# Expert values in two halves: one half of the columns as a dense product, the other gathered

## The reference, cut to what matters

```python
idx = jnp.take_along_axis(cand_idx, pos, axis=-1)      # i1 * 128 + i2
gate = jax.nn.softmax(top_s.astype(jnp.float32), axis=-1).astype(tb.dtype)
u = expert_u[idx]
v = expert_v[idx]
act = jax.nn.gelu(jnp.einsum('td,thkd->thk', tb, u), approximate=False)
return jnp.einsum('thk,thkd->td', gate * act, v)
```

## Time and profile before

| | |
|---|---|
| median of 3 runs | 1885.55 us (1879.7 to 1885.57) |
| profiled execution | 1886.42 us, span 1884.6 us |
| busy: TensorE, VectorE | 81%, 57% of the span |
| busy: GpSimd, ScalarE | 41%, 18% |
| bytes moved | 713 MB, 378 GB/s over the span |
| granted clock of TensorE, mean | 0.983 |

### The profile page before, as it was taken

How to read it: one execution, slowest core, us unless ns; L and a number is a source line. 1 busy time by engine, 2 the same in 40 slices (tenths; PEclk the granted TensorE clock), 3 DMA queues, 4 the chain that set the end, 5 groups by cost and what they waited for, 6 DMA issues and landing times.

```text
span 1884.6 us, 13048 instructions
## 1 busy us (share of the span) xinstructions
PE 1530.9 (81%) x4481; PEld 704.7 (37%) x4481; DVE 1075.2 (57%) x1518; ACT 331.4 (18%) x860; POOL 780.5 (41%) x666
## 2 busy tenths in 40 slices
PE   5989999999999677777777778777777777777775
PEld 3434564565459323223232323232232323232232
DVE  3127888776138846565564655553865555646445
ACT  3011211120122211211212121121221211111111
POOL 0002243311005585545555555452764545455441
PEclk8999999999999899999999999999999999999998
DMA  9998998885657999999999999999999999999997
GB/s 361 360 351 309 336 355 308 321 316 215 226 195 293 372 423 422 421 422 421 422 421 421 421 422 421 421 422 413 414 421 422 422 421 421 421 421 422 421 421 295
DMA packets 145008, 713.04 MB, mean 378 GB/s; under 512 B 14320, under 2 KB 16944, under 8 KB 77616
## 3 DMA queue, kind: packets, MB, share of 16 engines
q0 software_dynamic: 92160, 604.02, 78.2%
q1 hardware_dynamic: 52784, 108.20, 15.7%
HBM read 709.97 MB, written 2.20 MB: 378 GB/s over the span
## 4 chain that ended last, share of the span: by engine, by line
DMA 54%; PE 31%; DVE 6%; POOL 5%; issue 2%; SPq 1%; ACT 1%; DVEq 0%; POOLq 0%; ACTq 0%
DMA arena<-in_expert_v,arena 48%; PE PS L1558 6%; PE PS L1417 6%; POOL arena L505 5%; PE PS L1637 5%; PE PS L1319 5%; DMA arena<-in_expert_u,arena 5%; PE PS L1300 3%; DVE arena L1174 2%; PE PS L1275 1%; DMA arena<-in_w_in 1%; PE PS L1441 1%; DMA arena<-in_w_mod 1%; PE PS L1352 1%; SPq L340 1%
## 5 line engine op out<-in xcount | busy, mean ns | idle before, releaser
L1637 PE MATMUL PS<-arena 128*128 128x512 f32 x2016 | 942.0, 612 | 309.5 <-DMA arena<-in_expert_v,arena 309.5
L1174 DVE CUSTOM_DVE_ANT_0 arena<-arena 128x2048 f32<-128x2048 f32 x256 | 584.3, 2291 | 496.0 <-DMA arena<-in_expert_u,arena 495.4
L1637 PEld LDWEIGHTS PS<-arena 128*128 128x128 f32 x2016 | 368.5, 192 | 882.5 <-DMA arena<-in_expert_v,arena 505.7
L505 POOL DMA_INDIRECT arena<-in_expert_v,arena x256 | 370.0, 1445 | 446.8 <-PE PS L1637 413.3
L505 POOL DMA_INDIRECT arena<-in_expert_u,arena x256 | 313.3, 1224 | 241.7 <-DVE arena L1155 89.2
L798 ACT ACTIVATE arena<-arena 128x128 f32<-128x128 f32 x252 | 98.0, 402 | 770.3 <-PE PS L1637 769.5
L902 DVE SCALAR_TENSOR_TENSOR arena<-arena 128x1024 f32<-128x1024 f32 x120 | 161.1, 1342 | 26.8 <-DMA arena<-in_w_mod 24.0
L434 POOL DMA_DIRECT2D arena<-in_w_mod x128 | 68.6, 538 | 224.1 <-DVE arena L902 194.1
L1417 PE MATMUL PS<-arena 128*128 128x512 f32 x256 | 111.5, 593 | 0.0
L1558 PE MATMUL PS<-arena 128*128 128x512 f32 x256 | 110.9, 593 | 0.4 <-DVE arena L1076 0.4
L1319 PE MATMUL PS<-arena 128*128 128x512 f32 (+1 forms) x256 | 99.5, 547 | 4.2 <-DMA arena<-in_w_in 4.2
(11 more groups left out here) (207 smaller groups left out, 839.0 us busy)
## 6 DMA issues: line engine op xcount, KB each, us to landing
arena<-in_w_mod POOLq DMA_DIRECT2D x128, 512.0 KB, 6.9
arena<-in_w_mod SPq DMA_DIRECT2D x32, 1024.0 KB, 14.3
arena<-in_w_in SPq DMA_DIRECT2D x28, 1024.0 KB, 15.6
arena<-in_w_out SPq DMA_DIRECT2D x16, 1024.0 KB, 12.5
arena<-in_w_query SPq DMA_DIRECT2D x8, 1024.0 KB, 8.5
arena<-in_x SPq DMA_DIRECT2D x4, 1024.0 KB, 6.3
arena<-cum_rows SPq DMA_DIRECT2D x4, 1024.0 KB, 9.1
arena<-tail_rows SPq DMA_DIRECT2D x4, 1024.0 KB, 6.8
```

The costliest lines, as they stand in the source:

```text
L505: nc.gpsimd.indirect_dma_start(slot, None, table, bass.IndirectOffsetOnAxis(ap=idx[:, u % BUF, j:j + 1], axis=0),).then_inc(arrived, 16)
L1174: V.tensor_tensor_reduce(out=rows, in0=rows, in1=h2row[u // PH], scale=1.0, scalar=0.0, op0=ALU.mult, op1=ALU.add, accum_out=dots[:, u % B ...
L1637: ins = M(PS[:, 4 * blk + b, :], diag_slot[j % 8], vslot[m % NV][:, b * NQ:(b + 1) * NQ], start=first, stop=last)
```

## The change

The columns of expert_v are split into two halves of 1024 (4 KB of a row each).

*Right half, units 0 to 13 (224 slots, `N_DENSE`).* It is not gathered. For each token block a matrix G (128 x 128 x 128: first key index on the partitions, second key index i, token t) is built in SBUF. It holds for each expert and token the sum of the coefficients. Then the right half of the whole table is read once in 128 tiles (128 rows, one for each first index, of 4 KB: `tile_load`, by SyncE, four places), and TensorE multiplies each tile with G of both blocks (`all_experts`, four products of 128x512).

G is built for four tokens at a time, 32 batches for each block. For token t GpSimd makes a 0/1 matrix, slot by first key index (`first_halves`, four compares of 128x128), a second one, slot by second key index, holds the coefficient in place of 1, and TensorE multiplies them (`scatter`, one product of 128x128 for each token); ScalarE copies four results into G (`g_out`). The second matrix is made by ScalarE for block 0 (Abs, Relu and Copy with a scale) and by VectorE for block 1. Block 0's batches stand between dot products 146 and 208, one at every second; block 1's stand in one piece behind dot product 223, with coefficients and indices transposed by TensorE ahead of them.

*Left half, units 0 to 13.* Half rows of 4 KB are gathered. 96 of the slots go over TensorE as before, with two products each (86 of them spread from dot product 28 on, 9 for every 4 half rows, ten between block 1's batches, `V_LATE`). The other 128 are gathered in pairs and added by VectorE (`add_row`).

*Units 14 and 15.* Their rows of expert_u are gathered after G is done, in one ring of four places of 8 KB with the pairs; after them their whole rows of expert_v alternate with the other pairs (`ITEMS`). The ring runs beside the tiles. Unit 15 is routed only after block 1's batches.

*Other.* x after the mixing is stored to HBM and loaded again at tile 64; the last steps are rearranged in `close`; the loop of w_mod loads on GpSimd is written out; some semaphores are merged; one small product makes the numbers 1 to 128.

```diff
+HALF = D // 2
+BLK = PH * TOPK
+DENSE = UNITS - 2
+N_DENSE = DENSE * TOPK
+SLOTS = [BLK, N_DENSE - BLK]
+BATCH = 4
+BATCHES = P // BATCH
+V_SLOTS = 4
+TILES = 4
+LAST_TILES = 3
...
+V_SPREAD, V_PE = 86, 96
+V_AT = {n: [m for m in range(V_SPREAD) if 28 + 9 * m // 4 == n] for n in range(N_DENSE)}
+G_AT = {146 + 2 * b: b for b in range(BATCHES)}
+T_AT, T_MORE = 140, 214
+V_LATE = {1: [86, 87, 88, 89], 5: [90], 9: [91], 13: [92], 17: [93], 21: [94], 25: [95]}
+ITEMS = [x for i in range(2 * TOPK) for x in (("u", N_DENSE + i), ("pair", V_PE + 2 * i))]
+ITEMS += [x for i in range(2 * TOPK) for x in (("pair", V_PE + 4 * TOPK + 2 * i), ("full", N_DENSE + i))]
+N_RING = 4
```

The places in SBUF (offset in KB) and SyncE's list:

```diff
+        vslot = [at(64 + 4 * s, HALF) for s in range(V_SLOTS)]
+        bring = [at(k, D) for k in (152, 64, 72, 199)]
+        tile = [at(k, HALF) for k in (191, 195, 172, 178)]
+        acc = [at(168, HALF), at(160, D)]
+        G = [at(k, P * P).rearrange("p (i t) -> p i t", i=P) for k in (80, 0)]
+        oh1, oh2 = [[at(160 + 4 * a + 2 * b, BATCH * P).rearrange("p (t i) -> p t i", t=BATCH) for b in range(2)] for a in range(2)]
```

```diff
+            def tile_load(i):
+                if i == 0:
+                    sp.wait_ge(u_used, U_EARLY)
+                elif i == 2:
+                    sp.wait_ge(idx_ready, UNITS)
+                elif i == 3:
+                    sp.wait_ge(g_ps, 2 * BATCHES)
+                    sp.wait_ge(v_used, V_PE)
+                elif i >= TILES:
+                    sp.wait_ge(tile_used, i - TILES + 1)
+                src = expert_v.rearrange("(a b) n -> a b n", b=NKEYS)[:, i, HALF:D]
+                sp.dma_start(tile[i % TILES], src).then_inc(tile_in[i % TILES], 16)
+            for i in range(NKEYS):
+                tile_load(i)
+                if i == NKEYS // 2:
+                    grow_load(3)
+                    sp.wait_ge(dram_out, 80)
+                    for t in range(2):
+                        sp.dma_start(x1row[t], x1_dram[t * P:(t + 1) * P, :]).then_inc(grow_in, 16)
```

GpSimd:

```diff
             def gather_v(m):
                 if m == 0:
...
+                    pool.wait_ge(dram_out, 80)
+                if m >= V_SLOTS:
+                    pool.wait_ge(v_used, m - V_SLOTS + 1)
...
+            def item_load(k):
...
+                if kind == "pair":
+                    gather(expert_half, slot[:, 0:HALF], arrived, i, idx_left)
+                    gather(expert_half, slot[:, HALF:D], arrived, i + 1, idx_left)
+                else:
+                    gather(expert_u if kind == "u" else expert_v, slot, arrived, i)
+            def first_halves(b):
...
+                used = slice(0, SLOTS[blk])
+                for i in range(BATCH):
+                    ins = nc.gpsimd.tensor_scalar(oh1[b % 2][used, i, :], iota128[used], eT[used, 0, t + i:t + i + 1], None, ALU.is_equal)
+                ins.then_inc(oh1_ready, 1)
...
-            n = 0
-            for m in range(UNITS * TOPK):
-                while n < u_before(m):
-                    gather_u(n)
-                    n += 1
-                gather_v(m)
+            for n in range(N_DENSE):
+                gather_u(n)
+                for m in V_AT[n]:
+                    gather_v(m)
+                if n in G_AT:
+                    first_halves(G_AT[n])
+            item_load(0)
+            for b in range(BATCHES):
+                first_halves(BATCHES + b)
+                for m in V_LATE.get(b, []):
+                    gather_v(m)
+            for k in range(1, len(ITEMS)):
+                item_load(k)
```

ScalarE, block 0's second matrix and the copy into G:

```diff
+            def second_halves(b):
+                act.wait_ge(slots_evac, 2)
+                if b >= 2:
+                    act.wait_ge(g_ps, b - 1)
+                o = oh2[b % 2]
+                for i in range(BATCH):
+                    ins = A(o[:, i, :], iota128, ACT.Abs, bias=eT[:, 1, b * BATCH + i:b * BATCH + i + 1])
+                step(ins)
+                step(A(o, o, ACT.Relu, scale=-1.0, bias=1.0))
+                for i in range(BATCH):
+                    ins = A(o[:, i, :], o[:, i, :], ACT.Copy, scale=coefT[:, b * BATCH + i:b * BATCH + i + 1])
+                ins.then_inc(oh2_ready, 1)
+            def g_out(b):
+                blk, t = divmod(b * BATCH, P)
+                act.wait_ge(g_ps, b + 1)
+                A(G[blk][:, :, t:t + BATCH], PS[:, 6 + b % 2, :].rearrange("p (t i) -> p i t", t=BATCH), ACT.Copy).then_inc(g_evac, 1)
```

VectorE, block 1's second matrix, the adding of rows and the new order:

```diff
+            def second_halves(b):
...
+                    dve.wait_ge(slots_evac, 4)
+                dve.wait_ge(g_ps, b - 1)
+                for i in range(BATCH):
+                    ins = ts(oh2[b % 2][used, i, :], iota128[used], eT[used, 1, t + i:t + i + 1], coefT[used, t + i:t + i + 1],
+                             ALU.is_equal, ALU.mult)
+                ins.then_inc(oh2_ready, 1)
...
+            def add_row(m, row):
+                a = acc[m // BLK]
+                c = coef[:, m:m + 1]
+                if m == V_PE:
+                    dve.wait_ge(v_used, V_PE)
+                    ins = stt(a, row, c, PS[:, 0:2, :].rearrange("p b n -> p (b n)"), ALU.mult, ALU.add)
...
+                else:
+                    ins = stt(a, row, c, a, ALU.mult, ALU.add)
+                ins.then_inc(row_added, 1)
+                dve.wait_ge(row_added, ROWS.index(m) + 1)
+            def item(k):
...
-                if n == (PH + 1) * TOPK - 1:
-                    after_block(0)
-            after_block(1)
+            for b in range(BATCHES, 2 * BATCHES):
+                second_halves(b)
+            pick_keys(UNITS - 1)
+            pick_pairs(UNITS - 1)
+            for k in range(len(ITEMS)):
+                item(k)
...
+            dve.wait_ge(blk_done, 1)
+            close(0)
+            for h in range(2):
+                part = slice(HALF + h * NQ, HALF + (h + 1) * NQ)
+                dve.wait_ge(blk_done, 2 + h)
+                tt(acc[1][:, part], acc[1][:, part], PS[:, 4 + h, :], ALU.add).then_inc(right_added, 1)
+            dve.wait_ge(right_added, 2)
+            close(1)
```

TensorE:

```diff
             def expert_rows(m):
+                pe.wait_ge(v_in[m % V_SLOTS], 16 * (m // V_SLOTS + 1))
+                pe.wait_ge(coef_ready, m + 1)
+                for b in range(2):
+                    ins = M(PS[:, b, :], diag_slot[m % DIAGS], vslot[m % V_SLOTS][:, b * NQ:(b + 1) * NQ], start=(m == 0), stop=(m == V_PE - 1))
                 ins.then_inc(v_used, 1)
...
+            def scatter(b):
+                pe.wait_ge(oh1_ready, b + 1)
+                pe.wait_ge(oh2_ready, b + 1)
+                pe.wait_ge(g_evac, b - 1) if b >= 2 else pe.wait_ge(sc_evac, UNITS)
+                used = slice(0, SLOTS[b // BATCHES])
+                for i in range(BATCH):
+                    ins = M(PS[:, 6 + b % 2, i * P:(i + 1) * P], oh1[b % 2][used, i, :], oh2[b % 2][used, i, :], start=True, stop=True)
+                ins.then_inc(g_ps, 1)
+            def all_experts(i, blk):
+                for h in range(2):
+                    ins = M(PS[:, 2 + 2 * blk + h, :], G[blk][:, i, :], tile[i % TILES][:, h * NQ:(h + 1) * NQ], start=(i == 0), stop=(i == NKEYS - 1))
...
+                return ins
+            for n in range(N_DENSE):
+                if n == T_AT:
+                    slot_transposes(0)
+                    coef_transpose(0)
+                if n == T_MORE:
+                    slot_transposes(1)
+                for m in V_AT[n]:
                     expert_rows(m)
+                if n in G_AT:
+                    scatter(G_AT[n])
+            coef_transpose(1)
+            for b in range(BATCHES):
+                scatter(BATCHES + b)
+                for m in V_LATE.get(b, []):
+                    expert_rows(m)
+            pe.wait_ge(g_evac, 2 * BATCHES)
+            for i in range(NKEYS - LAST_TILES):
+                pe.wait_ge(tile_in[i % TILES], 16 * (i // TILES + 1))
+                all_experts(i, 0)
+                all_experts(i, 1).then_inc(tile_used, 1)
+            for blk in range(2):
+                for i in range(NKEYS - LAST_TILES, NKEYS):
+                    pe.wait_ge(tile_in[i % TILES], 16 * (i // TILES + 1))
+                    all_experts(i, blk)
```

More of the change, by code:

```diff
@@ L41 @@
 GR = 4
-NU = NV = 8
+NU = 8
 EARLY = 5
@@ L89 @@
 FIRST_KEYS_AFTER, FIRST_PAIRS_AFTER, FIRST_WEIGHTS_AFTER = 4, 9, 3
-LAST_ON_DVE = (8, 10, 12, 14)
-LAST_ON_PE = [j for j in range(TOPK) if j not in LAST_ON_DVE]
+WEIGHTS_AFTER = 15
 STATES = [(2, 0), (3, 0), (3, 1), (2, 1), (0, 0), (1, 1)]
@@ L440, in _ @@
                 tail_load(k % MORE_TAILS, 0, k)
-            with pool.Fori(1, 4) as half:
+            for half in range(1, 4):
                 for k in range(KT):
                     pool.wait_ge(tail_used, half * KT + (k - MORE_TAILS + 1))
-                    pool.sem_inc(pool_go, 1)
                     tail_load(k % MORE_TAILS, half, k)
@@ new lines, in _, with square @@
+            for u in range(DENSE):
+                unit(u)
+            coef_out(1)
+            for m in V_LATE[1]:
```

(31 more changed lines are left out.)

341 lines of the change are left out of this document (205 added, 136 removed).

## The result

The change makes the kernel slower: 2013.9 us (2005.3 to 2016.9, 4 runs) against 1885.6 us, a ratio of 1.068 with a 95% interval of 1.064 to 1.072. The forecast had the sign, the place and the two engines, and not the size: 1911 us, range to 1958. The profiled execution has a span of 2013.3 us.

A forecast was written before the change was run, and what follows sets the result against it. The full software DMA queue was taken to bound the kernel. With 98 us less to move (110 saved, 12 for 4 KB pieces) and 124 more idle, it came 25 us slower: 1911 us, own range 1892 to 1945, joined range 1812 to 1958.

The forecast's parts named there:

- Bytes: Whole kernel: about 46 MB or 110 us less to move; 4 KB pieces at about 410 GB/s cost 12 us.
- Stage A: First gather to dot product 28, before any expert_v: starts at 573.4, done at 666 us.
- B1: Dot products 28 to 145: VectorE sets 2.93 us each, against 3.06 of DMA; 346 us, to 1012.
- I take 3.9: Dot products 146 to 207, compares on GpSimd: 3.9 us each, between 3.06 and 4.3; 236 us, to 1248.
- Block 1's batches: Second token block's 32 batches, nothing streamed: compares 72 us, late half rows 28; 100 us, ends 60 and 115.
- The last stage: Tiles beside the ring: 484 us of transfers, ending at 1895; TensorE 443 us, not the bound by 41.
- Rival 2: Last stage, four-slot ring beside the tiles: queue not kept full, 4.3 us an item, +66, 1975 us; chance 0.10.
- Rival 1: GpSimd's compares find gaps in dot products 146 to 207 and block 1's batches: 1826 us; chance 0.40.
- the forecast's signs of being right: Dot products 146 to 207 at 3.7 us or more; batches near 100 us, share under 0.3; then 405 to 415 GB/s.
- B2: Dot products 146 to 207, with compares on GpSimd: 4.3 us each as upper end, 3.9 taken, 236 us.

The follow-up runs named there:

- e2: The kernel after, with block 0's compares made by VectorE instead of GpSimd: 1914.9 us.
- e1: The kernel after, with VectorE summing the row of expert_u alone (one SBUF input, not two) for dot products 146 to 207: 1958.4 us.
- e7: e2 with two of the four first compares of each block 1 batch moved from GpSimd to VectorE: 1899.9 us.
- e8: The kernel after with the edits of e2, e5, e6 and e7 together: 1871.8 us, ratio 0.995 to the kernel before.
- e5: e2 with all 96 half rows gathered before dot product 224, none between block 1's batches: 1892.1 us.
- e4: The kernel after, with small extra products on TensorE into an unused bank to keep it busy: 2008.9 us.
- e6: e2 with the tiles held back to the ring's pace, so both streams end together: 1913.5 us.
- e10: e8 with small extra products on TensorE, 16 behind each half row and four behind each block 1 batch: 1875.7 us, ratio 0.995 to the kernel before.

## Why the prediction failed in size

**Bytes, right.** In all 667 MB were moved where it was 713, the 46 MB less that were counted. The software queue fell from 604.0 to 486.6 MB by the half rows that are no longer gathered; the tiles, 67 MB, go through the other queue. It is chance that 486.6 is so near the forecast's 486.5: the software queue lacks the tiles and carries as many bytes of w_mod. 4 KB pieces in a mixture with 8 KB ran at 411 to 414 GB/s, where the forecast's shares of 410 and 421 give 414.

**Stage A right, B1 17 us short and set by the queue.** Dot product 28 is where it was forecast, the queue runs at 419. B1 took 363 us to the start of 146 instead of 346, and in e2, without these compares on GpSimd, the same 363. Dot products 16 to 31 came at VectorE's 2.91 us each, all from 48 on at 3.0 to 3.1: the rows in hand lasted for about two units and not for most of the stretch, and from there the full queue (share 1.02) set the pace, as the forecast's own 3.06 us of DMA says.

**The step that failed: "I take 3.9", dot products 146 to 207.** This is the term that was mis-sized. The place, the two engines and the lock were named, and e1 and e2 show them. The compare was priced at 0.3 us between bounds of 0.22 and 0.42, from a memset and an add of 16 elements; it takes 0.59 in the clear. And between ends of 3.06 and 4.3 a middle was taken, though 4.3 was what the argument itself gave. With 0.59 its own sum reads (3.6 + 2.4) / 2 + 1.8 = 4.8 us per dot product; measured are 4.76. This fit is in part luck: e1, without the lock, still takes 3.85 us per dot product and not 3.0, so the lock costs 0.9 of the 1.8, and the rest is compares that wait for TensorE and ScalarE, which the sum did not have. From dot product 144 to 208 the stretch lost 109 us against the 196 that the transfers need; moving the compares away gives back 94 (e2), lifting the lock from gathers and compares 56 (e1). How the other 38 us of e2's 94 divide between the compares' own length and these waits no run shows.

**Block 1's batches: right in length (113 against 103), wrong in one reason.** The forecast let GpSimd's and VectorE's compares take turns, 2.25 us a batch. They do not (e7, e8); GpSimd's four alone take 2.36. By luck the two errors cancelled. The late rows cost 37 us here (e5, beside e2) against the 28 set down; the products of one took 3.8 us at the low clock, against 1.8 in e4.

**The last stage.** The forecast had TensorE 41 us away from being the bound. It was busy for 431 of the 440 us to 1940, with a tile every 3.55 us, and the queue was full too (412 GB/s). The tiles ended first, and the ring had 52 us alone at 304 GB/s. Rival 2 named this ring and put 66 us on it for the whole stage; it costs 8 (e6) to 18 (all of the excess), at the end only.

**Rivals.** Rival 1 (compares find gaps) is refuted by the 1045 ns. Of the forecast's signs of being right, dot products of 3.7 us or more (4.76), a DMA share under 0.3 in the batches (0.15) and 405 to 415 GB/s beside the tiles (411) came. The error in this one stretch, 59 us, carried the sum beyond the range, because its upper end joined half of one rival to the forecast, and not the upper ends of the terms: B2's 4.3 alone gives 1911 + 25, and no term for a dearer compare was in it.

## What to carry to other kernels

Work moved to an idle engine has two prices, its own and what locks it out: here GpSimd's small compare cost 0.59 us, and 1.05 beside VectorE operations with two SBUF operands, while the busier VectorE did it in 0.24. Take bounds for an unseen small operation from the nearest small operation of the same engine and form, and if there is none, leave room for a factor of two. A saving of bytes is worth something only where transfers run: against 110 us less of them stood 109 us lost between dot products 144 and 208, and 113 with a DMA share of 0.15. Moving in-order waits out of that gap (e5, 37 us of it and 23 of the time) gave more than splitting its compares (e7, 18 and 15).

## What the runs showed of the hardware that was not expected

- A compare of 128x128 (tensor_scalar, fp32) takes GpSimd 0.59 us, where a memset of 2048 elements takes 1.8: by the memset's rate 128 elements would be 0.11 us. Compares of another length are in no run, so how much of the 0.59 is fixed is not shown.
- GpSimd's tensor_scalar and VectorE's, both on SBUF, ran side by side: GpSimd's took 0.60 to 0.62 us, VectorE's six of a batch 1.69 us against 1.51 alone (e8). The Trainium skill (SBUF — State Buffer, Who interferes with whom) says that a tensor_scalar in its two-port mode excludes GpSimd; whether VectorE's compare with two scalars runs in that mode is not shown, and no exclusion was seen. For operations with two SBUF inputs the Trainium skill's rule agrees with e1 (1045 against 622 ns).
- TensorE was granted 0.50, its 1.2 GHz level, all through block 1's batches in e8, while it worked in short pieces for 59 of the 65 us; with four more products behind each batch (e10) it was granted 0.94. In the kernel before it had 1.00 in the gather stage; in the kernel after it had 0.62 from 630 to 1017 us, about dot products 16 to 143, with TensorE busy for 46% of them.
